# Sums of squares as high and low part in rounded matmuls, at five norms of a two-block kernel

## The reference

```
def rmsnorm_2(x, g):
    xf = x.astype(jnp.float32)
    y = xf * lax.rsqrt(jnp.mean(xf * xf, axis=-1, keepdims=True) + EPS)
    return (y * g.astype(jnp.float32)).astype(x.dtype)
```

## Time and profile before

| | |
|---|---|
| median of 3 runs | 916.72 us (916.6 to 917.53) |
| the profiled execution | 917.72 us, of it 915.9 us span |
| PE (TensorE matmul) busy | 899.6 us, 7423 records |
| DVE busy | 642.4 us |
| ACT busy | 524.6 us |
| second mixer, first to last tile | about 549.8 to 705.3 us of the span |

### The profile page before, as it was taken

The page is one execution under the profiler, slowest core; times in us unless marked ns, Lnnn a source line. Parts: engine busy times, 40 slices in busy tenths (PEclk is TensorE's granted clock), DMA queues, the critical chain, the costliest instruction groups (busy, mean ns, idle before and its releaser), DMA issues.

```text
span 915.9 us, 18465 instructions
## 1 busy us (share of the span) xinstructions
PE 899.6 (98%) x7423; PEld 884.0 (97%) x7423; DVE 642.4 (70%) x1107; ACT 524.6 (57%) x868; POOL 4.7 (1%) x11
## 2 busy tenths in 40 slices
PE   8998999999999999999999999999999999999996
PEld 8998989999999999999999999999999999999996
DVE  6899887677556766666765647768669877767553
ACT  6898866676336655444444435544675665454452
POOL 1000000000000000000000000000000000000000
PEclk9999999999999999999999999999999999999999
DMA  9652435255765566555556565554315555665641
GB/s 325 219 171 90 138 119 181 86 192 185 242 199 170 192 208 191 171 170 177 177 173 202 164 181 160 161 164 138 139 59 195 185 185 187 201 194 199 212 138 47
DMA packets 110468, 157.63 MB, mean 172 GB/s; under 512 B 9772, under 2 KB 61104, under 8 KB 110256
## 3 DMA queue, kind: packets, MB, share of 16 engines
q1 hardware_dynamic: 109632, 154.96, 52.7%
q10 hardware_dynamic: 576, 0.96, 0.3%
q0 software_dynamic: 176, 0.53, 0.2%
HBM read 155.37 MB, written 1.05 MB: 171 GB/s over the span
## 4 chain that ended last, share of the span: by engine, by line
PE 91%; DVE 5%; ACT 1%; issue 1%; DMA 1%; SPq 0%; DVEq 0%; ACTq 0%
PE ps L1044 28%; PE ps L1046 28%; PE ps L1045 28%; DVE wl L1807 1%; PE ps L1127 1%; PE ps L1091 1%; DVE S L2210 1%; DMA raw<-d_small 1%; PE ps L1301 0%; PE ps L1321 0%; PE ps L1137 0%; PE ps L1259 0%; PE ps L1322 0%; PE ps L1281 0%; PE ps L1074 0%
## 5 line engine op out<-in xcount | busy, mean ns | idle before, releaser
L1807 DVE TENSOR_TENSOR wl<-raw,wh 128x1024 fp32r<-128x1024 f32 (+2 forms) x291 | 346.1, 1212 | 194.1 <-ACT wh L1380 193.7
L1380 ACT ACTIVATE wh<-raw 128x1024 fp32r<-128x1024 f32 (+2 forms) x291 | 298.4, 1046 | 190.6 <-PE ps L1046 190.2
L1044 PE MATMUL ps<-U,wh 128*128 128x256 f32 (+2 forms) x1392 | 397.7, 286 | 2.1 <-DVE wl L1807 2.1
L1046 PE MATMUL ps<-U,wl 128*128 128x256 f32 (+2 forms) x1392 | 391.2, 281 | 0.0
L1045 PE MATMUL ps<-UL,wh 128*128 128x256 f32 (+2 forms) x1392 | 390.5, 281 | 0.0
L1044 PEld LDWEIGHTS ps<-U,wh 128*128 128x128 f32 (+1 forms) x1392 | 262.4, 188 | 4.6 <-DVE wl L1807 2.5
L1045 PEld LDWEIGHTS ps<-UL,wh 128*128 128x128 f32 (+1 forms) x1392 | 262.5, 189 | 1.6 <-issue 1.0
L1046 PEld LDWEIGHTS ps<-U,wl 128*128 128x128 f32 (+1 forms) x1392 | 262.0, 188 | 0.0
L1044 PE MATMUL ps<-H,wh 128*128 128x256 f32 (+1 forms) x736 | 207.9, 282 | 0.0
L1046 PE MATMUL ps<-H,wl 128*128 128x256 f32 (+1 forms) x736 | 205.4, 279 | 0.0
L1045 PE MATMUL ps<-HLO,wh 128*128 128x256 f32 (+1 forms) x736 | 205.1, 279 | 0.0
(11 more groups left out here) (339 smaller groups left out, 790.1 us busy)
## 6 DMA issues: line engine op xcount, KB each, us to landing
raw<-w_ff SPq DMA_DIRECT2D x64, 512.0 KB, 4.4
raw<-ffn_w_gate SPq DMA_DIRECT2D x88, 256.0 KB, 3.7
raw<-ffn_w_up SPq DMA_DIRECT2D x88, 256.0 KB, 4.5
raw<-ffn_w_down SPq DMA_DIRECT2D x44, 512.0 KB, 4.4
raw<-w_in SPq DMA_DIRECT2D x40, 512.0 KB, 4.2
raw<-w_out SPq DMA_DIRECT2D x16, 512.0 KB, 3.7
raw<-wkv_x SPq DMA_DIRECT2D x8, 512.0 KB, 3.6
raw<-w_in SPq DMA_DIRECT2D x9, 256.0 KB, 3.2
```

What stands on the lines that cost most here:

```text
L1044: e.matmul(out, sh, xh, start=(i == 0 and n == 0), stop=False)
L1046: mm = e.matmul(out, sl, xh, start=False, stop=(over and n == nk - 1))
L1380: e.activation(wh, raw, ACT.Copy).then_inc(*up("w_hi", v))
L1807: lo = e.tensor_tensor(wl, raw, wh.bitcast(F32), ALU.subtract)
```

## The change

1. `rstd_sum` of ffn, f1, mix2 and f2: after the last of the eight adds, DVE copies `ACC` to a high part and subtracts that from `ACC` for the low part, both fp32r, in the two halves of `G`. TensorE sums both with two fp32r matmuls and waits for the low part.
2. `norm_sum` of og: ACT copies each half's squares (512 columns) to an fp32r tile `SQH` (step `norm_halves`, after both squares), DVE subtracts for `SQL`, and TensorE has two fp32r matmuls of 512 columns in place of each fp32 one. The letter `o` has two more steps, after its second.
3. The fp32r ones are made by one DVE copy of 128x128 in stage ffn, into the space of `RM`.
4. `gla_logits` uses 32 rows of its operands in place of 128 (the other rows of the weights are zero).
5. `ORDER_2` is a new string: 343 letters in place of 336 (two more `o`, four more `w`, one more `b`); the tiles are the same.

```
 ORDER_2 = (
-    "vvvvwvvviiiviiwiiviwviiivvgaivvvviiiiiaiiiiiiiaiVwiwViVigVgiiiaiigiggigaiiigggaiiiiwiVwgwgVgaxa0garg"
-    "r0rrwrkkgrwrr0rkkrrwrArrg0qqAr00r1wppggw1qggqgqgq21gpxg2ggwp1qggw2ggppgpggw1q3gpB30wgw2ggg1gw3gg3ggt"
-    "gwtgggB24wwA1CA4gt3B2D53C5B2CD4534CDg46D5351o6o7465gggogogggg7gowo64g77woog5g6oo7gg67bo567ow7ooobbbb"
-    "bwbbbbwwbbwbbbbbbbbbbbbwbwwbbtbwbbbb"
+    "viivvvwvviiviiwviiviwiiavgvwivvvvviiiiiiiiiwwigiaViiiViViwigiagwgViiigiiiiiaaggiigiagiwiwgaVwxag0gr"
+    "gagrrVwrrw0rrrkk00rrrwrrAkkrgqqArp0r1gq0gwg1ggqwq2qgpp1Bgppwg2gw1ggpgqBggxwgg1pg3wg2tw21gggt0qwggggw"
+    "gp3g3ggg3224gwA1wtA4CgBD3D5C3B2C4C3545DDg46535o16g5ooo7ggogw4gg7gogg67w67oogwogggbboo465677g657bow7b"
+    "oobwtooobbbbbwbbbwbbbbwbbbbwbbbbwbbbbwbbbbw"
 )
...
+        if tag == "og":
+            for i in range(n):
+                self.step("norm_halves", tag, i)
+                yield True
...
+        if tag in SUM_HALVES:
+            one = t["ONE"][:, :]
+            e.wait_ge(*at("sum", (tag, 9)))
+            e.matmul(pb, one, t["GR"][:, 0, 0:n], start=True, stop=False)
+            e.matmul(pb, one, t["GR"][:, 1, 0:n], start=False, stop=True).then_inc(*up("rstd_sum", tag))
+            return
...
+        if tag == "og":
+            one, hi = t["ONE"][:, :], t["SQH"][:, 512 * i:512 * i + 512]
+            e.wait_ge(*at("scaled", ("og", i)))
+            e.matmul(pb, one, hi, start=True, stop=False)
+            e.matmul(pb, one, t["SQL"][:, a:z], start=False, stop=True).then_inc(*up("norm_sum", (tag, i)))
+            return
...
-            e.matmul(bank(("gla_logits", i))[:, 0:T2], t["glagw"][:, 128 * i:128 * i + 128], GL, start=True,
+            e.matmul(bank(("gla_logits", i))[:, 0:T2], t["glagw"][0:32, 128 * i:128 * i + 128], GL[0:32, :], start=True,
...
+SUM_HALVES = ("ffn", "f1", "mix2", "f2")
...
+    def norm_halves(tag, i):
+        sq = norm_tiles(t, tag)[4]
+        e.wait_ge(*at("norm_square", (tag, i)))
+        e.activation(t["SQH"][:, 512 * i:512 * i + 512], sq[:, 512 * i:512 * i + 512], ACT.Copy).then_inc(
+            *up("norm_square", (tag, i, "high")))
...
+        if k == 1 and stage == "ffn":
+            e.tensor_copy(t["ONE"][:, :], cst("ones")).then_inc(*up("sum", ("ones", 0)))
+        if k == 7 and stage in SUM_HALVES:
+            hi, lo = t["GR"][:, 0, 0:n], t["GR"][:, 1, 0:n]
+            e.wait_ge(*at("sum", (stage, 7)))
+            e.tensor_copy(hi, acc).then_inc(*up("sum", (stage, 8)))
+            e.wait_ge(*at("sum", (stage, 8)))
+            e.tensor_tensor(lo, acc, hi.bitcast(F32), ALU.subtract).then_inc(*up("sum", (stage, 9)))
+
+    def norm_halves(tag, i):
+        sq = norm_tiles(t, tag)[4][:, 512 * i:512 * i + 512]
+        e.wait_ge(*at("norm_square", (tag, i, "high")))
+        e.tensor_tensor(t["SQL"][:, 512 * i:512 * i + 512], sq, t["SQH"][:, 512 * i:512 * i + 512].bitcast(F32), ALU.subtract).then_inc(
+            *up("scaled", ("og", i)))
...
+        t["SQL"] = nc.alloc_sbuf_tensor_at("SQL", [P, 1024], F32R, offset=at + 10 * SL * 4)
+        t["SQH"] = nc.alloc_sbuf_tensor_at("SQH", [P, 1024], F32R, offset=at + 11 * SL * 4)
...
+        t["GR"] = nc.alloc_sbuf_tensor_at("GR", [P, 2, T2], F32R, offset=at)
...
+        t["ONE"] = nc.alloc_sbuf_tensor_at("ONE", [P, P], F32R, offset=at)
```

More of the change, by code:

```diff
@@ L122 @@
 ORDER_2 = (
-    "vvvvwvvviiiviiwiiviwviiivvgaivvvviiiiiaiiiiiiiaiVwiwViVigVgiiiaiigiggigaiiigggaiiiiwiVwgwgVgaxa0garg"
-    "r0rrwrkkgrwrr0rkkrrwrArrg0qqAr00r1wppggw1qggqgqgq21gpxg2ggwp1qggw2ggppgpggw1q3gpB30wgw2ggg1gw3gg3ggt"
-    "gwtgggB24wwA1CA4gt3B2D53C5B2CD4534CDg46D5351o6o7465gggogogggg7gowo64g77woog5g6oo7gg67bo567ow7ooobbbb"
-    "bwbbbbwwbbwbbbbbbbbbbbbwbwwbbtbwbbbb"
+    "viivvvwvviiviiwviiviwiiavgvwivvvvviiiiiiiiiwwigiaViiiViViwigiagwgViiigiiiiiaaggigiigagiwiwgaVwxag0gr"
+    "gagrrVwrrw0rrrkk00rrrwrrAkkrgqqArp0r1gq0gwg1ggqwq2qgpp1Bgppwg2gw1ggpgqBggxwgg1pg3wg2tw21gggt0qwggggw"
+    "gp3g3ggg3224gwA1wtA4CgBD3D5C3B2C4C3545DDg46535o16g5ooo7ggogw4gg7gogg67w67oogwogggbboo465677g657bow7b"
+    "oobwtooobbbbbwbbbwbbbbwbbbbwbbbbwbbbbwbbbbw"
 )
@@ L1777, in act_program @@
         "split": split, "first_split": first_split, "first_square": first_square, "rstd": rstd, "store": store,
-        "rotary_tables": rotary_tables, "mem_split": mem_split, "evac": evac, "norm_square": norm_square,
+        "rotary_tables": rotary_tables, "mem_split": mem_split, "evac": evac, "norm_square": norm_square, "norm_halves": norm_halves,
         "norm_rs": norm_rs, "y_split": y_split, "latent_square": latent_square, "latent_rs": latent_rs,
@@ L2397, in dve_program @@
         "split": split, "zeroed": zeroed, "zeroed_again": zeroed_again, "first_split": first_split, "first_square": first_square, "angles": angles,
-        "rotary_tables": rotary_tables, "mem_split": mem_split, "evac": evac, "hidden_low": hidden_low,
+        "rotary_tables": rotary_tables, "mem_split": mem_split, "evac": evac, "hidden_low": hidden_low, "norm_halves": norm_halves,
         "scaled": scaled, "latent_square": latent_square, "latent_split": latent_split, "rope": rope,
@@ L2531, in build @@
                 t[f"SY{2 * j + i}"] = nc.alloc_sbuf_tensor_at(f"SY{2 * j + i}", [P, SL], F32, offset=at + j * SL * 4)
+        at = nc.sbuf_base
         t["S"] = sb("S", [P, 13 * SL])
+        t["SQL"] = nc.alloc_sbuf_tensor_at("SQL", [P, 1024], F32R, offset=at + 10 * SL * 4)
+        t["SQH"] = nc.alloc_sbuf_tensor_at("SQH", [P, 1024], F32R, offset=at + 11 * SL * 4)
         t["raw"] = sb("raw", [P, NRAW, SLOT])
```

## The result

The changed kernel takes **929.67 us** (median of 4 runs, 926.3 to 931.18), the kernel before 916.66 beside it: ratio 1.0135, 95% interval 1.0123 to 1.0146. The forecast was 915.9, in a range of 914.9 to 917.7. So the change costs 13 us where it was to save almost one. The profiled execution took 929.82, its span is 928.0 (before 917.72 and 915.9). Ratios here leave out a run that took over 1.5% more than the fastest of its kernel as a slow one; of the runs in the table further down these are one of kernel e (931.05) and one of kernel i (932.72), while their medians and ranges have them in.

A forecast was written before the change was run, and what follows sets the result against it. TensorE was taken as the bound from 170 us on. Products -1.69, mixer wait +0.75, og chain and rest +0.15 give -0.79 us from 916.72, so 915.9 us, range 914.9 to 917.7.

The forecast's parts named there:

- Together the products save 1.69 us: Four stage sums and two og sums: fp32r pairs in place of fp32 save 0.87 and 0.82 us.
- from 170 us on time follows the work on TensorE, one for one: Behind 170 us TensorE is always busy, so every new wait of it adds in full.
- The pairs themselves: Sums of ffn, f1, mix2, f2: two fp32r matmuls each save about 0.22 us, 0.87 us in all.
- The og sums: Two og sums: fp32r pairs of 512 columns at 0.45 us instead of 0.86, 0.82 us saved together.
- The wait at the mixer's start: New string puts six memsets ahead of gvr's third unit's split; TensorE waits 0.55 to 0.85 us, taken as 0.75.
- the 0.2 us forecast without high and low part: Mixer's start: without the high and low part the split comes some 0.5 us earlier, wait about 0.2.
- gla_logits: Gate logits over 32 rows: same columns and type, between 0.1 us gained and 0.1 lost, taken as 0.
- og chain and the rest of the string: First og sum waits 0 to 0.4 us, two other tight places 0 to 1.2; 0.15 us taken in all.
- No wait at ffn, f1, f2: DVE's low parts and splits there are ready in time: 0, with at most 0.15 us lost.
- The clock: Rival: behind the mixer's new wait the clock falls to 1.2 GHz, 1.7 us lost, 917.6; chance 0.06.
- The case of a pair that costs what fp32 costs: Rival: the rounded pairs cost the same as the fp32 sums, so 917.6 us; chance 0.08.

The follow-up runs named there:

- e: Changed kernel with the four stage sums' ones, high and low part moved to 320, 0 and 512 modulo 1024 bytes; 917.56 us, ratio 1.0029.
- i: Changed kernel with only the low part of the four stage sums moved, to 512 modulo 1024 bytes; 922.69 us, ratio 1.006.
- b: Kernel before with the og halves alone, two more `o` in the old string, and gate logits over 32 rows; 916.31 us, ratio 0.9993.
- l: Kernel before with the og halves alone and gate logits over all 128 rows; 916.68 us, ratio 0.9994.
- q: Kernel before's order with og halves, 128-row logits, pairs only in f1 and mix2 (parts in free tiles), fp32 at ffn and f2; 915.54 us, ratio 0.9991.
- o: Changed kernel with high and low part at 0 and 512, old string with two more `o`, logits over 128 rows; 916.33 us, ratio 1.0014.
- c: Changed kernel with the four stage sums back in fp32; 916.45 us, ratio 0.9997.
- f: Changed kernel with rounded pairs in f1 and mix2 alone, ffn and f2 in fp32; 917.79 us, ratio 1.0007.
- r: Kernel before, all sums fp32, plus one rounded 256-column product (ones at 448, stream at 384) behind ffn's and f2's sums; 930.97 us, ratio 1.0153.
- a: Kernel before with the four stage sums as rounded pairs and 32-row gate logits, og in fp32, old string; 923.38 us, ratio 1.0067.
- n: Changed kernel with each stage sum's two products swapped, low part first; 920.16 us, ratio 1.0038.
- bare stream: Not the computation: ff1a's gemm stream alone, no other engine at work, with fp32 sums, products or pairs inserted; 340 and 353 ns per three matmuls.
- the map: Gemm stream alone, rhythm set first, then one product at each of 16 stream addresses, ones at 448 or 320; 340 or 353 ns by address modulo 256.

## Why the prediction was wrong

- **The step that failed** is "Together the products save 1.69 us", read with the first part's "from 170 us on time follows the work on TensorE, one for one". I priced two matmuls by their own columns and took those around them as fixed. They were not: a pair whose low part streams from 384 left the stream in the 353 ns rhythm, at 6.5 and 6.8 us for two stretches (they are 6.30 and 6.60 longer, where the sum alone should have made each 0.2 shorter). That is 13.3 us; forecast and profile are 12.8 apart by their spans, and the smaller terms below make the difference. The kernel before shows both rhythms: the earlier trace rows has nine records in 1.07 us (119 ns), has 113, and from 131 us to stage x's sum at 148.9 its directly following 256-column matmuls are 117.8 ns apart in the mean. I used the rows for prices of columns and never asked why the 256-column distance had two values.
- **The pairs themselves**: 0.24 us instead of 0.44 for ffn, and the other three as much less, -0.20 each, forecast -0.22. The og sums 0.46 against 0.86, and 64.50 to 63.76 us from og to f2 (kernels b and l): -0.74, forecast -0.82. Right but for a tenth. In the string of before, mix2's saving doesn't last: from f1's to f2's sum q is 0.21 us shorter than l, o 0.20, which is one pair and not two. In q the low part is queued ahead of the memsets and a small split, and that split's tile starts 0.35 us behind its predecessor instead of 0.13.
- **The wait at the mixer's start** was sized too small. Its idle time is 0.76 us, but the forecast 0.75 was how much later the tile would start, and by starts that is 0.91 (1.03 less 0.12), with another 0.10 for the slow first matmul: 1.0 us. That the idle time reads 0.76 is a coincidence of two different quantities. Of the 0.2 us forecast without high and low part, c, which has the same string and fp32 sums, shows 0.27: no entry in its waits, but starts 0.28 and 0.23 apart at this tile. f, with the pairs, has 1.03 and 0.23 again.
- **gla_logits** was set to 0 within 0.1. It costs **0.40 us** more: from its first matmul to the next step 1.11 instead of 0.71 us, and l against b has it alone, 109.22 against 109.62. What it buys: the rows from 32 up of that tile now hold the rounded parts.
- **og chain and the rest of the string**: forecast 0.15. From f1's to f2's sum the changed kernel is 0.30 slower. The pairs give -0.40, og -0.74, the mixer's start 1.0, the logits 0.40, which leaves under 0.1 for these.
- **No wait at ffn, f1, f2**: right. TensorE's waits have one new entry, the 0.76. **The clock** stayed at 1.00 behind it.
- The first 1.15 us less belong to no edit: they are the stretch at 1.2 GHz shown above. mix's sum starts at 20.1 to 20.4 in the six profiles that have these 3.4 us, between 8 and 12.3 us, at 22.1 in r's, which has 6.8, and at 18.8 to 19.0 in the eleven that have none, of kernels that are the same up to there. That is a part of each kernel's spread of 1 to 2 us.
- Of the rivals none had this mechanism. The case of a pair that costs what fp32 costs came nearest in kind, with the price in the wrong place: 0.9 us in the pair, instead of 13 in what follows.

The Trainium skill (TensorE: Matmul & The Clock Gate, Part 1, section on 56 against 53.3 ns) has back-to-back matmuls, its example in bf16, at columns divided by 2.4 GHz plus some 2.5 ns. By that 256 columns would take an estimated 109.2 ns. The windows here have 113.2 and 117.6 in one and the same kind of fp32r stream at the same clock, so one price per column count, the Trainium skill's or mine, isn't enough.

**Open.** What in TensorE's reading of weights and stream makes two stable rhythms. And what besides the last inserted product decides in the full kernel: a lost only one stretch with the low part at 384, i lost one with it at 512, and e, n and o differ from run to run. The bare stream had nothing like it, but for the low part alone and the first group. It has neither the other engines' accesses nor the waits of a real stage; which of these acts was not tried. Nor did any run vary the PSUM bank or the length of the inserted product by itself.

## What to carry to other kernels

Where TensorE streams back to back for long, measure its start-to-start distance as records per window, before and after, and not only the edit's own instructions: 0.1 us of matmul put in cost 6 to 7 us over the next 170. Here an fp32 sum as the last interruption ahead of the long streams was the safe form: of the 102 runs of the kernel before and the 52 of b, c, f, l and q none is above 919.3. The addresses are the weaker means. With the operands of the inserted products at the stream's own, four of e's ten runs still lost a stretch or two; so read all runs, since one profile may show the good one of two outcomes. When a string or an order is written anew, count what now stands ahead of each weight split in the queue; the late tile of the mixer was foreseen by such a count, to within 0.3 us. And take what a wait costs from the distance of starts: here the idle time left a quarter of it out.

## What the runs showed of the hardware that was not expected

- Rounded 256-column matmuls in threes (two of one weight block, one of another) have two stable rhythms, 340 and 353 ns, with no other engine at work. Each lasted until something was inserted, in the full kernel for up to 180 us.
- In the bare stream, which one follows a single inserted product goes by its stream's address modulo 256 bytes and its weights' address, as in the map; in the full kernel this was a bias. An inserted product at the bare stream's own addresses left the rhythm as it was (16 of 16 with the ones at 320 and the stream at 0 or 64 modulo 256).
- An fp32 sum left 340 ns in all bare groups but the first, and in every ffn and f2 stretch that it was the last thing ahead of. A one-column fp32 matmul did not. Nor does an fp32 sum always: behind the one of stage x the rhythm is 353 in 13 of the 18 profiles, for the some 4 us until other matmuls follow. In 15 of the 18 TensorE comes to that sum late, 0.22 to 0.50 us behind the matmul before it; the late ones and the others have both outcomes.
- Four fp32 matmul records over 32 rows, among matmuls over 128, cost more than over 128:

```profile
L1231 PE MATMUL ps<-G,glagw 128*128 128x272 f32 x4 | 1.1, 391 | 0.0
```

```profile
L1247 PE MATMUL ps<-G,glagw 32*128 32x272 f32 x4 | 1.2, 414 | 0.0
```

The groups of the kernel before and after (busy us, mean ns) show only 23 ns a record of it; the starts show the 0.40 us. Between its other records the distance is 228 to 230 ns either way. It is longer at the ends: 208 instead of 115 ns ahead of the first record, 333 instead of 229 behind it, and from the last record to the second of what follows 0.55 instead of 0.35 us. So the extra time stands where the row count changes, and not in the 32 rows themselves.
